# Routed experts on one core: 32 tokens of each block by dots on fetched rows instead of 16, products of 352 columns, and a second selection over 80 sums per head

## What is computed

```python
def peer(xn, wq, keys, u, v):
    def block(xb):                       # 128 tokens; 4 blocks
        q = (xb @ wq).reshape(128, 8, 2, 64)
        s1 = einsum('thd,hnd->thn', q[:, :, 0], keys[:, 0])   # 8 heads x 128 keys
        s2 = einsum('thd,hnd->thn', q[:, :, 1], keys[:, 1])
        v1, i1 = top_k(s1, 16)
        v2, i2 = top_k(s2, 16)
        cand = (v1[..., :, None] + v2[..., None, :]).reshape(128, 8, 256)
        sc, ci = top_k(cand, 16)
        e = i1[ci // 16] * 128 + i2[ci % 16]                  # one of 16384 experts
        g = softmax(sc)
        hid = einsum('thkd,td->thk', u[e], xb)
        a = gelu(hid) * g
        return einsum('thk,thkd->td', a, v[e])
```

## Time and profile before

| | |
|---|---|
| median of 3 runs | 3048.91 us (3048.26 to 3049.45) |
| profiled execution, span from first to last instruction | 3047.4 us |
| PE busy | 3023.7 us, 99% |
| DVE, ACT, POOL busy | 1871.5, 1146.5, 1924.1 us (61%, 38%, 63%) |
| hidden stage of the experts | about 1894 to 2517 us from the span's start |
| value stage of the experts | about 2519 to 3042 us |
| granted PE clock | full in all of the span's slices |

### The profile page before, as it was taken

The page is one execution under the profiler, slowest core; times in us unless marked ns, Lnnn a source line. Parts: engine busy times, 40 slices in busy tenths (PEclk is TensorE's granted clock), DMA queues, the critical chain, the costliest instruction groups (busy, mean ns, idle before and its releaser), DMA issues.

```text
span 3047.4 us, 42832 instructions
## 1 busy us (share of the span) xinstructions
PE 3023.7 (99%) x15259; PEld 2557.7 (84%) x15259; DVE 1871.5 (61%) x3350; ACT 1146.5 (38%) x2075; POOL 1924.1 (63%) x1812
## 2 busy tenths in 40 slices
PE   8999999999999999999999999999999999999999
PEld 7877888888668888888777888999999998888887
DVE  7674544316865442250663236989978858877786
ACT  3455322102553221120554212443367763333333
POOL 7423766677337666776433566698975576776763
PEclk9999999999999999999999999999999999999999
DMA  7211222222212222222112222699989999999995
GB/s 237 72 42 42 90 97 97 97 97 104 77 42 104 97 97 97 97 104 97 70 56 70 76 97 98 218 329 320 336 304 329 331 355 385 383 363 359 357 369 196
DMA packets 175166, 547.65 MB, mean 180 GB/s; under 512 B 13667, under 2 KB 67076, under 8 KB 155140
## 3 DMA queue, kind: packets, MB, share of 16 engines
q1 hardware_dynamic: 117348, 338.81, 32.4%
q0 software_dynamic: 39168, 142.62, 12.3%
q10 hardware_dynamic: 18464, 63.70, 5.7%
HBM read 487.55 MB, written 57.40 MB: 179 GB/s over the span
## 4 chain that ended last, share of the span: by engine, by line
PE 95%; ACT 2%; DVE 2%; issue 1%; POOL 1%; DMA 0%; ACTq 0%; DVEq 0%; POOLq 0%
PE banks L194 83%; PE banks L2946 2%; PE banks L2227 1%; PE banks L2265 1%; PE banks L1142 1%; PE banks L1229 1%; PE banks L2244 1%; PE banks L2867 1%; PE banks L1788 0%; PE banks L1826 0%; PE banks L1211 0%; PE banks L1804 0%; PE banks L1201 0%; POOL weights_split L3509 0%; PE banks L1748 0%
## 5 line engine op out<-in xcount | busy, mean ns | idle before, releaser
L194 PE MATMUL banks<-memory,weights_split 128*128 128x512 f32 (+1 forms) x9456 | 2044.4, 373 | 9.8 <-DVE memory L578 8.3
L194 PEld LDWEIGHTS banks<-memory,weights_split 128*128 128x128 f32 x9456 | 1693.2, 188 | 281.1 <-issue 33.1
L3674 POOL TENSOR_SCALAR weights_split<-weights_raw 128x512 fp32r<-128x512 f32 x576 | 376.7, 664 | 757.8 <-issue 382.8
L3679 POOL TENSOR_TENSOR weights_split<-weights_raw,weights_split 128x512 fp32r<-128x512 f32 x576 | 768.8, 1347 | 0.2
L3509 POOL TENSOR_TENSOR weights_split<-weights_raw,weights_split 128x512 fp32r<-128x512 f32 x384 | 507.4, 1345 | 269.4 <-ACT weights_split L3308 267.8
L194 PE MATMUL banks<-weights_split,memory 128*128 128x512 f32 (+1 forms) x2880 | 646.4, 386 | 0.0
L194 PEld LDWEIGHTS banks<-weights_split,memory 128*128 128x128 f32 x2880 | 533.8, 188 | 108.8 <-issue 1.0
L3308 ACT ACTIVATE weights_split<-weights_raw 128x1024 fp32r<-128x1024 f32 x256 | 268.6, 1051 | 43.4 <-DMA weights_raw<-in_weights 25.1
L712 DVE TENSOR_TENSOR banks<-banks,memory 128x512 f32<-128x512 f32 x88 | 61.3, 699 | 231.9 <-PE banks L194 231.8
L3026 DVE CUSTOM_DVE_ANT_0 memory<-memory,banks 128x1024 f32<-128x1024 f32 x144 | 172.4, 1212 | 34.2 <-DMA memory<-in_peer_u,memory 34.2
L3503 POOL DMA_INDIRECT memory<-in_peer_v,memory x128 | 161.8, 1264 | 41.0 <-issue 25.7
(11 more groups left out here) (305 smaller groups left out, 2730.4 us busy)
## 6 DMA issues: line engine op xcount, KB each, us to landing
weights_raw<-in_weights SPq DMA_DIRECT2D x143, 1024.0 KB
weights_raw<-in_weights SPq DMA_DIRECT2D x257, 512.0 KB
routing<-memory ACTq DMA_DIRECT2D x12, 2048.0 KB
hidden<-memory ACTq DMA_DIRECT2D x62, 384.0 KB
memory<-hidden SPq DMA_DIRECT2D x31, 768.0 KB
memory<-routing SPq DMA_DIRECT2D x30, 768.0 KB
window_rows<-memory ACTq DMA_DIRECT2D x1, 3064.0 KB, 27.5
chunk_rows<-memory ACTq DMA_DIRECT2D x1, 2556.0 KB, 13.3
```

What stands on the lines that cost most here:

```text
L194: last = k.nc.tensor.matmul(out, left[a], right[b], start=start and n == 0, stop=stop and n == 2, skip_group_check=True)
L3674: k.nc.gpsimd.tensor_scalar(cut(high, n * PIECE, PIECE), cut(raw, n * PIECE, PIECE), 1.0, 1.0, ALU.mult, ALU.mult).then_inc(k.high_made, 1)
L3679: k.nc.gpsimd.tensor_tensor(cut(low, n * PIECE, PIECE), cut(raw, n * PIECE, PIECE), cut(high, n * PIECE, PIECE).bitcast(F32), ALU.subtract ...
```

## The change

What it does:

- 32 instead of 16 tokens of the dense blocks go by dots, so a dense product has 352 columns, there are 160 dots, and 16 more rows are fetched.
- The second selection takes 80 sums per head instead of 256: 16 for the best row, 8 for each of the next seven, one for each of the last eight. Three additions make them, and seven small instructions instead of three turn a place among 80 into row and column. Some small tables move from SBUF to PSUM.
- All meeting points move: scores, turns, tokens, factors and the first matrix come at earlier units, and the matrices lie behind 46 units, not 34. `IN_ROUTE` is [0, 20, 24, 26]. 10 dots lie between the last selection and `weigh_picked`, 4 between that and the first one-hot.
- POOL's plan follows other marks.
- There are two buffers for the choices that are turned, so a wait for an earlier turn falls away for block 2.

```diff
-    PICKED, GROUPS = 16, P // 16
+    PICKED, GROUPS = 32, P // 32
...
-    SCORE_AT, EXP_AT, TURN_AT = [0, 8, 20, 46], [10, 32, 54, 76], [None, 39, 72, 82]
-    MATRIX_FIRST, MATRIX_COUNT = 84, 34
-    IN_ROUTE, IN_MATRIX, BEFORE_GATES = [0, 28, 27, 26], 51, 12
-    PICKED_AT, NUMBERS_AT, SUMS_AT, PLACE_AT = 52, 42, 43, 75
-    TOKENS_AT, GELU_AT, FACTORS_AT = 53, 74, 79
-    STEP_TIMES = [32, 116, 148, 193, 201, 224, 252, 315, 343, 375, 378, 382, 405, 428, 451, 474, 497, 520]
+    SCORE_AT, EXP_AT, TURN_AT = [0, 8, 18, 36], [8, 24, 42, 61], [None, 31, 67, 70]
+    MATRIX_FIRST, MATRIX_COUNT = 72, 46
+    IN_ROUTE, BEFORE_FACTORS, BEHIND_FACTORS, BEFORE_GATES = [0, 20, 24, 26], 10, 4, 12
+    IN_MATRIX = DOTS - sum(IN_ROUTE) - BEFORE_FACTORS - BEHIND_FACTORS - BEFORE_GATES
+    RUN, SUMS = 8, 80
+    PICKED_AT, NUMBERS_AT, SUMS_AT, PLACE_AT = 38, 33, 34, 75
+    TOKENS_AT, GELU_AT, FACTORS_AT = 40, 67, 69
+    STEP_TIMES = [32, 116, 148, 193, 201, 211, 227, 260, 276, 294, 302, 305, 310, 313, 336, 359, 382, 405, 428, 451]
...
-        marks = [(10, 0), (35, 28), (58, 55), (81, 81), (117, 132), (125, DOTS), (PEER_KEYS + 3, DOTS),
+        marks = [(10, 0), (28, 20), (46, 44), (65, 70), (72, 84), (118, 148), (124, DOTS), (PEER_KEYS + 3, DOTS),
                  (PEER_KEYS + SPARSE_END, ROWS)]
...
+            def add_pairs(at, first, rows, column, columns):
+                shape = [P, PEER_HEADS, rows, columns]
+                out = sums3[:, :, at:at + rows * columns].rearrange("p h (r c) -> p h r c", c=columns)
+                return v.tensor_tensor(out, best4[:, :, 0, first:first + rows].unsqueeze(3).broadcast_to(shape),
+                                       columns3[:, :, column:column + columns].unsqueeze(2).broadcast_to(shape), ALU.add)
...
-            ranked(PEER_HEADS, TOPK * TOPK, sums[0], sums[1], picked, pick)
...
-            v.tensor_scalar(row_col[:, 0:P].bitcast(U32), pick.bitcast(U32), 4, None, ALU.logical_shift_right)
-            then(v.tensor_scalar(row_col[:, P:2 * P].bitcast(U32), pick.bitcast(U32), 15, None, ALU.bitwise_and))
-            then(v.tensor_copy(row_col_f, row_col.bitcast(U32)))
-            if r >= 2:
-                dve.wait_ge(turned_up, r - 1)
+            add_pairs(0, 0, 1, 0, TOPK)
+            add_pairs(TOPK, 1, RUN - 1, 0, RUN)
+            then(add_pairs(SUMS - RUN, RUN, RUN, 0, 1))
+            ranked(PEER_HEADS, SUMS, sums[0], sums[1], picked, pick, True)
+            place = pick.bitcast(U32)
+            v.tensor_scalar(best_columns.bitcast(U32), place, RUN - 1, None, ALU.bitwise_and)
+            v.scalar_tensor_tensor(out=far_column, in0=place, scalar=float(TOPK), in1=place, op0=ALU.is_lt, op1=ALU.mult)
+            then(v.tensor_scalar(best_rows.bitcast(U32), place, 3, None, ALU.logical_shift_right))
+            then(v.scalar_tensor_tensor(out=last_row, in0=place, scalar=float(SUMS - RUN), in1=best_columns.bitcast(U32),
+                                        op0=ALU.is_ge, op1=ALU.mult))
+            v.scalar_tensor_tensor(out=best_rows, in0=best_rows.bitcast(U32), scalar=1.0, in1=last_row, op0=ALU.max,
+                                   op1=ALU.add)
+            then(v.tensor_tensor(best_columns, best_columns.bitcast(U32), last_row, ALU.subtract))
+            then(v.tensor_tensor(best_columns, best_columns, far_column, ALU.max))
+            if r >= 3:
+                dve.wait_ge(turned_up, r - 2)
...
             route(r)
             if r == 0:
                 make_masks()
+        consume(BEFORE_FACTORS)
         weigh_picked()
+        consume(BEHIND_FACTORS)
...
-                ahead = 4 if unit < 34 else 5 if unit < 70 else 6
-                goal = planned(unit - 3) + ahead if unit > 13 else 0
+                ahead = 4 if unit < 27 else 5 if unit < 57 else 6
+                goal = planned(unit - 3) + ahead if unit > 12 else 0
```

More of the change, by code:

```diff
@@ L2626, in expert_layer @@
         scores = [k.take(lists * P), k.take(lists * P)]
-        sums = [k.take(PEER_HEADS * TOPK * TOPK) for _ in range(2)]
+        sums = [k.take(PEER_HEADS * SUMS) for _ in range(2)]
     with k.scope(at=B_AT):
@@ L2636, in expert_layer @@
         picked, pick, shifted, exped_s = (k.take(PEER_HEADS * TOPK) for _ in range(4))
-        row_col, row_col_f, chosen = k.take(2 * P), k.take(2 * P), k.take(3 * P)
+        far_column, last_row = k.take(P), k.take(P)
+        choices = [k.take(3 * P) for _ in range(2)]
         match = k.take(PEER_HEADS * TOPK * TOPK)
-        total, inverse = k.take(8), k.take(8)
     with k.scope(at=X_AT):
@@ L2696, in expert_layer @@
     numbers, picked_hid, picked_factor, group_mask, token_mask = (
-        cut(common.work[2], at, size) for at, size in ((0, PICKED), (16, PICKED), (32, PICKED), (48, GROUPS), (64, PICKED)))
+        cut(common.work[2], n * PICKED, size) for n, size in enumerate((PICKED, PICKED, PICKED, GROUPS, PICKED)))
+    total = cut(common.work[2], 448, PEER_HEADS)
     chooser, all_numbers, spread, placed = (cut(common.work[3], n * P, P) for n in range(4))
@@ L2929, in turn_choices @@
             for n in range(3):
-                last = k.nc.tensor.transpose(score_banks[0].memory[:, n * P:(n + 1) * P], chosen[:, n * P:(n + 1) * P],
+                last = k.nc.tensor.transpose(score_banks[0].memory[:, n * P:(n + 1) * P], choices[r % 2][:, n * P:(n + 1) * P],
                                              k.const("ident"))
@@ L3106, in route @@
             step, left, counting = [0], [IN_ROUTE[r]], [IN_ROUTE[r] > 0]
-            sparse_block = ORDER[r] == DENSE_BLOCKS
+            sparse_block, chosen = ORDER[r] == DENSE_BLOCKS, choices[r % 2]
             def then(instruction):
@@ L3128, in ranked @@
                 then(last)
+                if shifts:
+                    v.tensor_copy(largest.unsqueeze(2), top.rearrange("p (n r) -> p n r", r=TOPK)[:, :, 0:1])
                 for n in range(count):
@@ L3139, in ranked @@
                 then(last)
+            def add_pairs(at, first, rows, column, columns):
[3 more added lines that the diff above has]
+                                       columns3[:, :, column:column + columns].unsqueeze(2).broadcast_to(shape), ALU.add)
+            by_head = [P, PEER_HEADS, TOPK]
+            sums3 = sums[0].rearrange("p (h n) -> p h n", h=PEER_HEADS)
+            columns3 = best_cols.rearrange("p (h r) -> p h r", h=PEER_HEADS)
             dve.wait_ge(copied, 4 * r + 4)
@@ L3143, in route @@
             ranked(lists, P, scores[0], scores[1], best, index)
-            v.tensor_copy(best_cols.rearrange("p (h r) -> p h r", h=PEER_HEADS), best4[:, :, 1, :])
-            v.tensor_copy(ranks_row, k.const("iota")[:, 0:TOPK])
+            v.tensor_copy(columns3, best4[:, :, 1, :])
             then(v.tensor_copy(index_f, index.bitcast(U32)))
-            then(v.tensor_tensor(sums[0].rearrange("p (h r c) -> p h r c", h=PEER_HEADS, r=TOPK),
-                                 best4[:, :, 0, :].unsqueeze(3).broadcast_to(quad),
-                                 best_cols.rearrange("p (h r) -> p h r", h=PEER_HEADS).unsqueeze(2).broadcast_to(quad),
-                                 ALU.add))
```

22 lines of the change are left out of this document (12 added, 10 removed).

## The result

The change takes 3118.8 us (median of 4 runs, 3115.3 to 3121.7) against 3049.1 us: ratio 1.0228, interval 1.0216 to 1.0240. It is slower by 2.3%, where 0.6% was forecast; 3118.8 lies 35 us above the range. The profiled execution has a span of 3113.5 us, 66.1 us more than before.

The account below looks back on a forecast made before the run. PE was taken to bound the kernel. Terms -26.0 + 26.7 (meetings) + 12 (matrices) + 3.2 (end) + 1 (first gates) = +16.9 us on 3047.4, plus 1.5 to the median's basis: 3066 us, range 3040 to 3084.

Parts of the forecast that it names:

- PE sheds 26 us: PE's hidden stage: narrower products -20.4 us, regrouped matrices -4.7, a vanished wait for POOL -0.9; sum -26.0 us.
- The selection: On DVE: the shorter second selection saves about 7 us per block, worth nothing by itself since DVE has cover.
- 1 to 6: New PE waits at meetings with DVE or POOL, from unit 28 to the first matrix: +26.7 us in sum.
- tokens: Ahead of unit 40: PE waits for the tokens, which need DVE's sums ahead of dot 34; +3.9 us.
- low parts between unit 28 and the factors: Units 49 to 68: POOL's 27 fetches in 19 units outlast PE's work, so low parts come late; about +2.4 us.
- first matrix: Behind unit 72: PE waits for the one-hot table and scalings, which stand behind dots 80 to 83; +8.2 us.
- The matrices, +12 (0 to 17.5): 46 units with matrices: scalings, tables, copies and late rows make PE wait; +12 us, from above 17.5.
- R3: Rival: transfers at their limit in the stage's second half, landings of 8 us or more, waits feeding each other; 3082 us, chance 0.07.
- R4: Rival: PE's clock falls to 1.2 GHz behind the larger two gaps, costing 6 us; 3072 us, chance 0.05.
- The end, +3.2: Last units, from 121 on: two fetches in each unit make POOL slower than PE; +3.2 us (0 to 5).
- A dot, 1.14 us: DVE's time for one dot, used to date the meetings: 1.14 us.
- R2: Rival: rows land in 5 us or selections are some 8 us shorter, so most meeting waits vanish; 3031 us, chance 0.16.

Follow-up runs that it names:

- e4: Only the change's 80-sum selection, its PSUM tables and second buffer, with 16 tokens by dots, 368 columns and the earlier kernel's tables: 3048.1 us.
- e1: On the changed kernel, POOL's goal from unit 74 on is 9 rows beyond the plan, not 6: 3067.6 us.
- e6: On the changed kernel, everything retimed (first matrix at unit 78, 9 rows ahead from unit 79), with 32 tokens and 352 columns kept: 3033.9 us.
- e8: On the kernel before the change, POOL's goal from unit 86 on is 2 rows beyond the plan, not 6: 3181.3 us.
- e10: On e6, 6 rows ahead to the end, as in the change, not 9: 3078.1 us.
- e2: On the changed kernel, tokens, factors, last turn and first matrix come three units later, rows as in the change: 3122.9 us.

## Why the prediction was wrong

The direction was right, the size not: +16.9 us forecast on the span, +66.1 measured.

- *PE sheds 26 us*: right. The pitch is 160 ns, though some 7 us of the account stay without a term.
- *The selection*: right. A find over 80 columns takes 235 ns, as worked out, and e4 shows that by itself it gives nothing.
- *1 to 6, the meetings*: five of six places were right. Unit 28: 2.0 us (3.1 forecast); tokens 8.5 (3.9); low parts between unit 28 and the factors 1.7 (2.4); factors 5.6 (6.5); unit 72 none (1.4); first matrix 8.4 (8.2). The tokens were mis-sized, since `take_numbers` took 6.5 us and not 0.9. DVE of the changed kernel:

```profile
2064.90 3.02 DVE L3078 TENSOR_TENSOR memory<-memory,memory 128x128 f32<-128x128 f32 x1
2067.95 0.37 DVE L3080 TENSOR_REDUCE memory<-memory 128x32 f32<-128x128 f32 x1
2068.36 3.06 DVE L3082 CAST memory<-memory 128x32 uint32<-128x32 f32 x1
```

  Before, the first took 0.29 us and the last, with 16 columns, 0.17. POOL made low parts from 2065.22 for 2.54 us and from 2068.89 for 2.48, and each of the two ends within 0.2 us of the end of a pair of low parts. This is the contention of the earlier trace rows, which I had priced for the selection (there it is gone: its last step takes 0.29 us in all four blocks) and not for this place. The Trainium skill ("GPSIMD Engine Reference", § 1 Specifications) names VectorE instructions with two SBUF inputs, which fits L3078, and those in a 2-port mode; L3082 has one input, and no run here tells what mode it is in.
- *The matrices, +12 (0 to 17.5)*: this is the step that failed. I asked if each engine had time enough in 5.62 us, and it has: e1 and e6 run such units with 0.2 and 1.4 us of waits at matrices behind the first in all. I took a row's landing (7.1 us) as the only delay and never compared, in the trace of before, how many rows lay between fetch and dot: four at unit 90, 2.8 on average. The loop over ACT's and POOL's queues made 32.9 us of waits out of a lead of 0.3 rows. R3 had described the loop (a late dot holds the next fetch, and with it the low part) with a chance of 0.07, and laid it to full transfers. They were emptier than before on average and full only in bursts. Landings did pass R3's 8 us (9.9 us for the dots that waited), but e1, e8 and e10 show that the lead decides, and with the clock the price was more than R3's 16 us.
- *R4, the clock*: the mechanism is real, and its size at the meetings about right: 6 us priced, 11.0 us of busy PE at the lower level there, so some 5.5. What it left out are the loop's shorter gaps: 32.5 us at the lower level in the matrix phase, some 16 us more. The forecast itself had the clock at nothing.
- *The end, +3.2*: 4.8 us of waits for low parts, within its 0 to 5. (Its sum is of seven units, 121 to 127, though the text names 123 to 127.)
- *A dot, 1.14 us*: the earlier trace rows shows 1.21, its duration. The 1.14 is the step from one dot to the instruction behind it, and the right number for dates.
- *R2, faster*: the landings from 2100 to 2243 us, of dots that waited, were 6.9 to 10.2 us (mean 8.1), not 5. It needed other dates, not other landings.

Added up: waits at meetings and low parts 31.0 us (29.9 were forecast for 1 to 6 and the end), in the loop 32.9 (12), clock some 22 (0). The error of 49 us is, to the nearest, 21 us of waits in the loop, 16 of the clock that it pulled down, 5.5 of the clock at the meetings, and the 7 us without a term. What stays open: why e8 is so much worse than the change (92.6 us against 32.9). Its average lead is the lowest, which fits, but no run shows how the waits grow with it.

## What to carry to other kernels

Where a queue issues a transfer behind work that itself waits for that transfer's consumer, lead is not slack but what keeps a loop from closing (three rows of it were worth 51 us in e1): count the items between issue and use in the old trace, and again under the new plan, before counting busy time. A gap of a few microseconds on TensorE costs more than itself, since the clock stays low behind it (5.54 us instead of 4.09 for the 24 products behind the factors). When a measure upstream brings nothing (e2), look for a loop downstream before dropping it.
